# First norm's weight applied at the copies of turned tiles, a longer idle block at the front, and a reordered third norm

## The reference, cut to what matters

```
def rms_norm(x, gain, eps=EPS):
    xf = x.astype(jnp.float32)
    y = xf * lax.rsqrt(jnp.mean(xf * xf, axis=-1, keepdims=True) + eps)
    return (y * gain.astype(jnp.float32)).astype(x.dtype)

h = rms_norm(x, pre_norm_gain[i])
proj = h @ w_in[i]
q, k, v, z_a, b_gate, c_gate, u, z_c = jnp.split(proj, N_IN_PARTS, axis=-1)
```

## Time and profile before

| What | Value |
|---|---|
| Time before, median of 3 runs | 873.04 us (872.52 to 873.81) |
| Profiled execution, its own time | 872.48 us |
| Its span, first to last instruction | 870.7 us |
| TensorE busy | 861.4 us, 99% |
| VectorE, ScalarE, GpSimd busy | 571.8, 391.0, 482.0 us |
| DMA | 106.84 MB, mean 123 GB/s |

### The profile page before, as it was taken

One profiled execution on the slowest core, in us unless ns is written; L12 is line 12 of the kernel. 1 busy time (PEld: TensorE's weight loads), 2 busy tenths in 40 slices (PEclk: granted clock), 3 DMA queues, 4 the chain that ended last, 5 costly groups with the idle time before them and its releaser, 6 DMA issues.

```text
span 870.7 us, 11938 instructions
## 1 busy us (share of the span) xinstructions
PE 861.4 (99%) x4196; PEld 717.9 (82%) x4196; DVE 571.8 (66%) x924; ACT 391.0 (45%) x836; POOL 482.0 (55%) x540
## 2 busy tenths in 40 slices
PE   8999999999999999999999999999999999999997
PEld 6888888888888788888888888888888988888885
DVE  6126647965997489776765635556997487798624
ACT  4123433423667377546112321113787446667622
POOL 7766555682217722318976038871324997666362
PEclk9999999999999999999999999999999999999999
DMA  7543222353871468994742262525973222112202
GB/s 201 166 123 97 76 73 73 119 138 83 218 238 53 141 142 179 218 220 165 167 123 97 63 203 79 140 96 121 235 176 98 73 97 74 49 49 74 73 1 96
DMA packets 83691, 106.84 MB, mean 123 GB/s; under 512 B 11953, under 2 KB 54449, under 8 KB 83634
## 3 DMA queue, kind: packets, MB, share of 16 engines
q1 hardware_dynamic: 72752, 85.12, 30.3%
q0 software_dynamic: 10880, 20.97, 14.2%
q10 hardware_dynamic: 2, 0.00, 0.0%
HBM read 103.98 MB, written 2.10 MB: 122 GB/s over the span
## 4 chain that ended last, share of the span: by engine, by line
PE 97%; ACT 1%; POOL 1%; DMA 0%; DVE 0%; issue 0%; DVEq 0%; POOLq 0%; ACTq 0%
PE bank L2222 29%; PE bank L2223 29%; PE bank L2224 29%; PE bank L2319 2%; PE bank L2466 2%; PE bank L2494 1%; PE bank L2439 1%; PE bank L2489 1%; PE bank L2488 1%; PE bank L2430 1%; PE bank L2429 1%; PE bank L2434 1%; POOL ms L830 0%; PE bank L2411 0%; DMA gain<-in_pre_norm_gain 0%
## 5 line engine op out<-in xcount | busy, mean ns | idle before, releaser
L880 POOL TENSOR_TENSOR wlo<-raw,whi 128x512 fp32r<-128x512 f32 x180 | 248.5, 1413 | 6.1 <-PE bank L2319 5.2
L871 POOL TENSOR_SCALAR whi<-raw 128x512 fp32r<-128x512 f32 x170 | 117.8, 733 | 171.0 <-PE bank L2224 162.0
L2222 PE MATMUL bank<-actB_hi,whi 128*128 128x512 f32 (+1 forms) x416 | 159.7, 384 | 0.0
L2223 PE MATMUL bank<-actB_lo,whi 128*128 128x512 f32 (+1 forms) x416 | 158.6, 381 | 0.0
L2224 PE MATMUL bank<-actB_hi,wlo 128*128 128x512 f32 (+1 forms) x416 | 158.5, 381 | 0.0
L2222 PE MATMUL bank<-whi,actA_hi 128*128 128x512 f32 x350 | 138.2, 395 | 0.8 <-DVE actA_lo L1518 0.7
L2224 PE MATMUL bank<-whi,actA_lo 128*128 128x512 f32 x350 | 136.4, 390 | 0.0
L2223 PE MATMUL bank<-wlo,actA_hi 128*128 128x512 f32 x350 | 136.3, 389 | 0.0
L2224 PEld LDWEIGHTS bank<-actB_hi,wlo 128*128 128x128 f32 x416 | 78.2, 188 | 15.2
L2222 PEld LDWEIGHTS bank<-actB_hi,whi 128*128 128x128 f32 x416 | 78.2, 188 | 15.1 <-issue 0.6
L2223 PEld LDWEIGHTS bank<-actB_lo,whi 128*128 128x128 f32 x416 | 78.3, 188 | 14.1
(11 more groups left out here) (275 smaller groups left out, 1640.5 us busy)
## 6 DMA issues: line engine op xcount, KB each, us to landing
raw<-in_a_w_in SPq DMA_DIRECT2D x44, 512.0 KB, 4.4
raw<-in_w_in SPq DMA_DIRECT2D x32, 512.0 KB, 3.9
raw<-in_b_w_in SPq DMA_DIRECT2D x16, 512.0 KB, 3.3
raw<-in_a_w_out SPq DMA_DIRECT2D x12, 512.0 KB, 3.4
gain<-in_a_w_out POOLq DMA_DIRECT2D x9, 512.0 KB, 8.9
raw<-in_w_ple_gate SPq DMA_DIRECT2D x8, 512.0 KB, 5.1
gain<-in_a_w_in POOLq DMA_DIRECT2D x8, 512.0 KB, 7.4
raw<-in_a_w_in POOLq DMA_DIRECT2D x8, 512.0 KB, 7.2
```

What stands on the lines that cost most here:

```text
L871: pool.tensor_scalar(H, src[:, i * HALF:(i + 1) * HALF], 1.0, 1.0, ALU.mult, ALU.mult).then_inc(w_hi, 1)
L880: ins = pool.tensor_tensor(L, src[:, i * HALF:(i + 1) * HALF], H.bitcast(f32), ALU.subtract)
L2222: M(out_, whi_, xhi_, start=start, stop=False)
L2223: M(out_, whi_, xlo_, start=False, stop=False)
```

## The change

Six edits:

1. The two `gn` blocks and the second `warm` block go. The first `warm` block has eight products instead of two.
2. The norm's weight is loaded as columns, 1,024 elements of 4 bytes, into the same tile.
3. `normed_x` multiplies only with 1/rms. The weight is multiplied in where turned tiles are copied: `turned_x` on ScalarE makes four copies of 128 columns, each with a column of the weight as scale, and `rest_x` on VectorE makes four rests in the same way. Each signals after its fourth.
4. GpSimd makes the root of h3 tile 2 ahead of that of "a" tile 3, and ScalarE squares in that order.
5. VectorE waits for the root of h3 tile 2 between the two halves of `lo_two` for k5.
6. `Fa` k5 0 waits for the first weight half only, and for the second where its fifth step needs it.

```diff
@@ -196,7 +196,7 @@
 def tensor_order():
 
     o = []
-    o += [("warm", 0)] + [("gn", c) for c in range(2)] + [("warm", 1)]
+    o += [("warm", 0)]
     for t in range(T):
         o += [("tr", "x", t, j) for j in range(2)]
         o += [("T", "v", 0, 0, t - 2)] if t >= 2 else []
@@ -282,7 +282,7 @@
         return BANKS_A[UNITS_A[b[1]][0]] + b[2]
     if kind == "s4":
         return 4 * (b[1] // 2 % 2) + b[1] % 2
-    return {"gn": lambda c: (7, 3)[c], "warm": lambda n: 6, "sc": lambda i, m: 4 + m, "tw": lambda i: 6, "pv": lambda i: 7, "ta": lambda h: IN_TURN.index((h,)) % 4,
+    return {"warm": lambda n: 6, "sc": lambda i, m: 4 + m, "tw": lambda i: 6, "pv": lambda i: 7, "ta": lambda h: IN_TURN.index((h,)) % 4,
             "ple": lambda t, c: (4, 5, 0, 1, 2, 3, 6, 7)[2 * t + c], "wt": lambda j: 4 + j, "rw": lambda j: 6 + j,
             "v5": lambda t: 4 + t % 2, "s5": lambda s, m: 4 + m, "t5": lambda s, kt: 6 + kt,
             "o5": lambda s: 3}[kind](*b[1:])
@@ -601,7 +601,7 @@
             a = b[1]
             if kind == "t5":
                 return (pt_lo[1], a + 1) if b[2] else (pt_lo[0], kt0_steps(a))
-            return {"gn": (tok_ready["x"], 7 + a), "sc": (scored, 2 * a + b[-1] + 1), "tw": (wt_copied, a + 1),
+            return {"sc": (scored, 2 * a + b[-1] + 1), "tw": (wt_copied, a + 1),
                     "pv": (attn_copied, a // 4 + 1), "ta": (attn_out, a + 1),
                     "ple": (e_copied, 2 * a + b[-1] + 1), "wt": (wct_copied, a + 1),
                     "rw": (rw_copied, a + 1), "s4": (s4_scaled, a + 1), "v5": (v5_lo, a + 1),
@@ -948,7 +948,7 @@
             after[at("u4", 5, 1)] = [lambda: add_a(5)]
             after[at("u4", 7, 1)] = [lambda n=n: add_a(n) for n in (7, 8, 9, 12, 13)]
             after[at("u4", 7, 1)] += [lambda n=n, t=t: root(n, t, D) for n, t in (
-                ("a", 0), ("a", 1), ("h3", 0), ("h3", 1), ("a", 2), ("a", 3), ("h3", 2), ("h3", 3))]
+                ("a", 0), ("a", 1), ("h3", 0), ("h3", 1), ("a", 2), ("h3", 2), ("a", 3), ("h3", 3))]
             for n in range(2 * len(UNITS)):
                 if n // 2 not in SPLIT:
                     continue
@@ -996,20 +996,31 @@
                 for c in range(1 if t < 2 else 2):
                     square("x", t, c, resid[:, t, c * HALF:(c + 1) * HALF])
 
-            act.dma_start(gain[0:1, 1], pre_norm_gain[0:1, :]).then_inc(gain_in[0], 16)
+            def turned_x(t, j):
+                b = ("tr", "x", t, j)
+                act.wait_ge(gain_in[0], 16)
+                act.wait_ge(pe_block, BLOCK[b])
+                bank = psum[bank_of(b)][:, :]
+                for k in range(4):
+                    ins = A(actA_hi[:, 4 * j + k, t * P:(t + 1) * P], bank[:, k * P:(k + 1) * P], ACT.Copy,
+                            scale=gain[:, 1, 4 * j + k:4 * j + k + 1])
+                ins.then_inc(hi["x"], 1)
+
+            with nc.allow_non_contiguous_dma(reason="columns of a gain, 4 KB"):
+                act.dma_start(gain[:, 1, 0:KD], pre_norm_gain[0].rearrange("(f p) -> p f", p=P)).then_inc(gain_in[0], 16)
             square_x(0)
             act.wait_ge(raw_in[0], LANDED[0, 0])
             A(halves_of(0, 0, 2)[0], raw[:, 0, :], ACT.Copy).then_inc(w_hi, 2)
-            turned("x", 0, 0)
+            turned_x(0, 0)
             square_x(1)
-            turned("x", 0, 1)
+            turned_x(0, 1)
             square_x(2)
-            turned("x", 1, 0)
+            turned_x(1, 0)
             square_x(3)
-            turned("x", 1, 1)
+            turned_x(1, 1)
             for t in range(2, T):
                 for j in range(2):
-                    turned("x", t, j)
+                    turned_x(t, j)
 
             act.wait_ge(lam_step, 2)
             A(lams[:, 2:4], lams[:, 0:2], ACT.Exp).then_inc(lam_exp, 1)
@@ -1439,8 +1450,8 @@
             turned_n(1)
             hi_k5(0)
             hi_k5(1)
+            h3_out(2)
             square_a(3, 0)
-            h3_out(2)
             normed_n(2)
             v5_out(0)
             h3_out(3)
@@ -1551,25 +1562,33 @@
                     dve.wait_ge(pe_block, BLOCK["tr", "x", t - 2, 1])
                 for c in range(2):
                     half = slice(c * HALF, (c + 1) * HALF)
-                    dve.wait_ge(pe_block, BLOCK["gn", c])
-                    V.scalar_tensor_tensor(tok[:, t % 2, half], resid[:, t, half], rstd[:, NORMS["x"], t:t + 1],
-                                           psum[bank_of(("gn", c))][:, :], ALU.mult, ALU.mult)\
+                    V.tensor_scalar(tok[:, t % 2, half], resid[:, t, half], rstd[:, NORMS["x"], t:t + 1], None, ALU.mult)\
                         .then_inc(tok_ready["x"], 1)
+
+            def rest_x(t, j):
+                dve.wait_ge(gain_in[0], 16)
+                dve.wait_ge(hi["x"], 2 * t + j + 1)
+                bank = psum[bank_of(("tr", "x", t, j))][:, :]
+                for k in range(4):
+                    at = (slice(None), 4 * j + k, slice(t * P, (t + 1) * P))
+                    ins = V.scalar_tensor_tensor(actA_lo[at], bank[:, k * P:(k + 1) * P], gain[:, 1, 4 * j + k:4 * j + k + 1],
+                                                 actA_hi[at].bitcast(f32), ALU.mult, ALU.subtract)
+                ins.then_inc(lo["x"], 1)
 
             square_x(0)
             normed_x(0)
             square_x(1)
-            rest("x", 0, 0)
-            rest("x", 0, 1)
+            rest_x(0, 0)
+            rest_x(0, 1)
             normed_x(1)
-            rest("x", 1, 0)
+            rest_x(1, 0)
             normed_x(2)
-            rest("x", 1, 1)
-            rest("x", 2, 0)
+            rest_x(1, 1)
+            rest_x(2, 0)
             normed_x(3)
-            rest("x", 2, 1)
-            rest("x", 3, 0)
-            rest("x", 3, 1)
+            rest_x(2, 1)
+            rest_x(3, 0)
+            rest_x(3, 1)
             dve.wait_ge(small_in, 16 * 13)
             for n in range(2):
                 V.tensor_tensor_reduce(lamv[:, 2 * n], lamv[:, 2 * n], lamv[:, 2 * n + 1], 1.0, 0.0,
@@ -2090,8 +2109,9 @@
             part_gain(2, 0)
             rest_n(1)
             h3_in(2)
-            for h in range(2):
-                lo_two(UNIT_NO["k5", 0], h)
+            lo_two(UNIT_NO["k5", 0], 0)
+            dve.wait_ge(rstd_ready["h3"], 3)
+            lo_two(UNIT_NO["k5", 0], 1)
             part_gain(3, 0)
             h3_in(3)
             v5_rest(0)
@@ -2226,7 +2246,7 @@
             def weights_of(stage, j, first_half=False):
                 n = UNIT_NO[stage, j]
                 if n in TWO_NO:
-                    pe.wait_ge(w7_lo, 2 * TWO_NO[n] + 2)
+                    pe.wait_ge(w7_lo, 2 * TWO_NO[n] + (1 if first_half else 2))
                 else:
                     pe.wait_ge(w_lo, 2 * SPLIT[n] + (1 if first_half else 2))
                 return whi[:, SLOT[n], :], wlo[:, SLOT[n], :]
@@ -2234,7 +2254,8 @@
             def feature_major(kind, stage, f):
 
 
-                H, L = weights_of(stage, f // 2)
+                by_half = kind == "Fa" and f == 0
+                H, L = weights_of(stage, f // 2, by_half)
                 aH, aL = READS[stage]
                 tokens = slice(0, S)
                 if stage == "k5":
@@ -2243,6 +2264,8 @@
                 out_ = psum[bank_of(("F", stage, f))][:, tokens]
                 first, last = (0, KD // 2) if kind == "Fk" else (KD // 2 * ((stage, f) in JOBS2), KD)
                 for k in range(first, last):
+                    if by_half and k == KD // 2:
+                        weights_of(stage, f // 2)
                     c = slice(k * 256 + (f % 2) * P, k * 256 + (f % 2) * P + P)
                     ins = exact(out_, H[:, c], L[:, c], aH[:, k, :], aL[:, k, :], k == 0, k == KD - 1)
                 return ins
@@ -2406,12 +2429,10 @@
                 bank = psum[bank_of(b)]
                 if kind == "tr":
                     return turn(*b[1:])
-                if kind == "gn":
-                    pe.wait_ge(gain_in[0], 16)
-                    return M(bank[:, :], ones[0:1, :], gain[0:1, 1, b[1] * HALF:(b[1] + 1) * HALF], start=True, stop=True)
                 if kind == "warm":
-                    for n in range(2):
-                        ins = M(bank[:, n * P:(n + 1) * P], ident[:, :], ones[:, :], start=True, stop=True)
+                    for n in range(8):
+                        c = slice(n % 4 * P, (n % 4 + 1) * P)
+                        ins = M(bank[:, c], ident[:, :], ones[:, :], start=True, stop=True)
                     return ins
                 if kind in ("F", "Fa", "Fk"):
                     return feature_major(*b)
```

## The result

The changed kernel takes 877.82 us (median of 4 runs, 877.54 to 878.13), the kernel before 872.78 us on the same chip (872.35 to 873.81): ratio 1.0062, interval 1.005 to 1.0074. It is slower, by 5.0 us where 2.8 were forecast, and inside the forecast range. The profiled execution took 877.85 us, its span is 876.1 us: 5.4 us more than before.

What follows compares the result with a forecast made beforehand. TensorE, busy 99% of the span, was taken as the bound. A front loss of 3.4 us less 0.6 us gained near 670 us gave +2.8 us: 875.8 us against 873.04, range 872.8 to 879.2 us.

Steps and rivals of the forecast that it cites:

- What leaves TensorE: Front: without gain products and second idle block, transposes start at 6.8 us, 1.1 us earlier; the longer idle block costs nothing.
- What the copies cost: Turned tiles, per half-tile: four pieces take 1.20 us instead of 0.60 on ScalarE, 1.17 instead of 0.69 on VectorE.
- cheap-copies rival: Front: pieces overlap more, so the kernel is not slower, down to 871.8 us; chance 0.19 without a difference, 0.06 faster.
- Tile by tile: Front: following the copies through the engines, 1.6 us lost at tile 1 and 1.8 us at tiles 2 and 3, 3.4 in all.
- the first term: Tile 1: its head block starts at 15.8 us instead of 14.22, 1.6 us later.
- Stalls at tiles 2 and 3: Before the head blocks of tiles 2 and 3: TensorE stands 0.9 us each time, 1.8 us in all.
- The gain's load: Front: the weight's columns land at 4.2 us, 3.6 us before ScalarE needs them, so the load is hidden.
- The rival of late columns: Front: the gain's pieces land at 12 us and ScalarE waits, 4.2 us lost, 880.0 us; chance 0.17.
- Clock: Front: TensorE's pauses delay the rise to 2.4 GHz, costing 0.4 to 1.8 us, 876.2 to 877.6 us; chance 0.08.
- The second place: Near 670 us: the reordering removes TensorE's 0.5 us gap and some 0.1 us at the next transposes, 0.6 us gained.
- The sum: Whole kernel: 3.4 us lost at the front less 0.6 us gained near 670 us, +2.8 us.

Runs made afterwards that it cites:

- e8: The changed kernel with an idle block of two products instead of eight: 878.61 us, ratio 1.0062 to the kernel before.
- e11: The kernel before with edits 4 to 6, eight idle products ahead of the gain products instead of two, no second idle block: 873.43 us, ratio 1.0014.
- e2: The changed kernel with one copy and one rest of 512 columns per half-tile, the norm's weight left out: 874.95 us, ratio 1.0032 to the kernel before.
- e5: The kernel before with an extra, unneeded load of the gain as 1,024 four-byte pieces, queued behind the gain's row load: 872.42 us, ratio 0.9999.
- e7: The kernel before with edits 4 to 6 and without its second idle block: 872.42 us, ratio 1.0.
- e12: The kernel before with edits 4 to 6, eight idle products first, no second block, eight more behind tile 0's transposes: 873.2 us, ratio 1.0017.
- e4: The changed kernel with 14 idle products at the front and 8 behind tile 0's transposes: 875.83 us, ratio 1.0046 to the kernel before.
- e6: The changed kernel with the gain loaded as eight rows of 512 bytes and turned by TensorE: 877.22 us, ratio 1.0044 to the kernel before.
- e9: The changed kernel with the gain as turned rows and eight idle products more behind tile 0's transposes, copies by pieces: 876.11 us, ratio 1.0043 to the kernel before.
- e3: The kernel before with an extra, unneeded load of the gain as 1,024 four-byte pieces, queued ahead of the gain's row load: 874.84 us, ratio 1.0032.
- e1: The kernel before with edits 4 to 6 alone: 871.49 us against 871.90, ratio 0.9994.

## Why the prediction came out as it did

**What leaves TensorE: right.** The transposes started at 6.74 us (forecast 6.8), and the idle block of 3.67 us cost nothing: it ended 1.3 us before they started, and with the short block of e8 they started at 6.78. What the early start is worth no run isolates; e11's 0.4 us left 0.06.

**What the copies cost: right.** Four pieces took 1.12 to 1.16 us on ScalarE (forecast 1.20) and 1.11 to 1.13 us on VectorE (forecast 1.17). So the cheap-copies rival had no ground.

**Tile by tile: the mechanism right, the first term too small.** This is the mis-sized term: head 1 was forecast 1.6 us late and was 2.9 us late. Its path was right up to the norm of tile 1, which was to start at 12.1 us; it started at 12.57, and two things came together there, both left out.

The one that came last is GpSimd's root. The prediction had it "at most 0.2 us off", which holds only with weights in time. Before, GpSimd's two weight rests ended at 10.15 us, its root of tile 1 at 11.30, and the norm started at 11.34. In the changed kernel the rests began 1.35 us later with the late weights, ended at 11.48 us, and the root at 12.54. So the norm could not start earlier, whatever VectorE did: in e2 VectorE was free and waited 1.00 us for the root. The rows of before:

```profile
7.19 2.96 POOL L880 TENSOR_TENSOR wlo<-raw,whi 128x512 fp32r<-128x512 f32 x2 [0.91 <-ACT whi L1002]
...
10.73 0.57 POOL L833 TENSOR_TENSOR rstd<-ms,mhalf 128x1 f32<-128x1 f32 x1
...
11.34 1.41 DVE L1555 SCALAR_TENSOR_TENSOR tok<-resid,rstd,bank 128x512 f32<-128x512 f32 x2
```

The other, VectorE's own rests, ended at 12.44 us, just ahead of the root. ScalarE was busy with the late weights until 8.3 us, so its first group began at 8.31 us, not 7.85. And the first rest began at 10.29 us, not 9.11, though ScalarE's group had ended at 9.44. VectorE was held by the square of x1, 1.78 us long instead of 0.85. GpSimd's pair of weight rests had started 0.04 us earlier. Undisturbed, that pair takes 2.5 us, 1.25 each. Add 1.25 to its start at 8.54: 9.79 us, and the square ended 0.57 us later, at 10.36. Other kernels give nearly the same. In before the pair started at 7.19 and the square ended at 9.02 us, 0.58 us after the pair's first instruction. In e5 it was 7.16 and 8.97, 0.56 after it. In e7 the square came in beside the pair's second instruction:

```profile
8.36 1.60 DVE L1545 CUSTOM_DVE_ANT_0 acc<-resid 128x512 f32<-128x512 f32 x1 [0.79 <-DMA resid<-in_x]
```

```profile
6.90 2.51 POOL L880 TENSOR_TENSOR wlo<-raw,whi 128x512 fp32r<-128x512 f32 x2 [0.77 <-ACT whi L1002]
```

There 6.90 plus 2.51 is 9.41, and the square ended at 9.96: 0.55 after it. In e12 it began behind both (9.95 us) and took 0.68 us. In these five the square moves only when GpSimd's instruction is through; GpSimd loses too, 2.94 us for the pair instead of 2.5. The Trainium skill, SBUF — State Buffer, "Who interferes with whom", says that a VectorE operation with both inputs in SBUF and a GpSimd operation that reads SBUF exclude each other; by that rule, the trace agrees (the square reads one half of x as both inputs). I had weighed that section for the norm alone. The norm's two halves did take 1.60 us at 12.57 us, against 0.88 alone at 6.20 us. The first half, for which 0.6 us were estimated, took 0.85 instead of 0.49: 0.4 more. It ended at 13.42 us and the transposes started at 13.47. TensorE's last product of tile 0 started at 12.90 us, and the ones at 1.2 GHz are spaced by 0.42, so without the longer half they could have started near 13.3: it cost some 0.1 us (an estimate from these rows).

The third part of the 1.3 us is the clock: tile 0's products and tile 1's transposes at 1.2 GHz. So the 1.3 us are, in order: 0.5 at the norm's start, 0.4 up to the transposes, and 0.4 to 0.5 on them. In the profiles, e4 (clock) and e6 (weights) each give 0.9 us at head 1, e4 with weights 0.44 us earlier besides, and e6 in its fastest run. In the times neither stands clear of the changed kernel. Both together (e9) gave no more at head 1, but e9 has the overlong fill: its norm of tile 1 started at 12.48 us, behind rests that the late transposes had delayed. So how the two add up stays open.

**Stalls at tiles 2 and 3: right.** 0.74 and 0.68 us of wait; from head 1 to head 3 the lag grew from 2.9 to some 4.9 us, 2.0 where 1.8 was forecast. e2, with whole copies, has no such stall.

**The gain's load: the cover held, the price was wrong.** It landed 5.1 us after issue, at 5.9 us, forecast 4.2, and ScalarE never waited. The sentence that its cover hides it looked only at who waits for this load. It should have asked whom it delays: the weights by 1.4 us, by e3, e6 and the throughput rows, and with them GpSimd's rests and its root. The rival of late columns was one queue place away (e5).

**Clock: a rival that came true beside the forecast.** I gave it 0.08 as a case of its own, at 0.4 to 1.8 us. It cost 0.5 to 0.9 us (e4's profile). The longer block raised the clock to where there was little to do. TensorE then stood 1.3 us before tr 0 and 1.66 us behind it, and products at 9.49 us ran at 1.2 GHz.

**The second place: right.** Forecast 0.6 us. In the changed kernel's trace its lag falls by 0.8 us at 670 us and grows by 0.2 at 675; e1 has 0.6. The 0.2 is tile 3, which the prediction had 0.3 us early: GpSimd's root of "a" tile 3 met the second weight rest (the 1.85 us above), and TensorE waited 0.22 us.

**The sum.** In the profiled execution: 2.9 (head 1) + 2.0 (tiles 2 and 3) - 0.6 (670 us) is 4.3 us. The span grew by 5.4. The remaining 1.1 us came, all but 0.1, in two steps near 255 and 279 us, with waits of 0.26 and 0.27 us for weight rests and for VectorE's `resid`. e4, e6 and e9 have nothing of the size there. Nor has e8, the changed kernel but for the idle block; its profile has 0.7 us near 380 us instead, and so have e3 (1.1) and e7 (0.7), while the changed kernel has none there. So steps of this size come and go at several places, with the front changed and without. Whether those of 255 and 279 us belong to the change stays open. Four runs of the changed kernel agree within 0.6 us, so it isn't one odd execution.

## What to carry to other kernels

Ask of a new small load whom it delays, not only who waits for it, and in which place of the queue it stands; then follow the delayed load through every engine in turn, here to a root on GpSimd that no edit had touched. When a copy between TensorE and its next block grows, count the gap and then the clock behind the gap. A late load shifts one engine's work into another's: look at what two engines start at the same moment on the same memory.

## What the runs showed of the hardware that I had not expected

- 1,024 pieces of 4 bytes, issued first, took away 0.42 MB of throughput between 3.2 and 5.2 us (36 GB/s in the worst slice, against 364). Issued 0.55 us later and behind another load, they landed after 11.3 us instead of 5.1.
- A clock raised by idle products had fallen again at the products of 9.49 us, after TensorE had stood for 1.3 and 1.66 us. Six idle products more in front and eight between brought 1.97 us down to 1.29 for the same eight transposes (e4).
- The clock column can print 1.00 where the products run at 1.2 GHz: in e6 it does for 10 to 15 us, with eight transposes in 1.97 us. The duration of a known shape is the better gauge.
